# One-hot routing table: eight tokens per operation, gates in two parts, two single-pass products per token

## The reference

```
expert = take_along_axis(i_top[0] * 128 + i_top[1], pos)      # 128 experts per token (8 heads x 16)
gate   = softmax(best)
a = gelu(einsum('td,ted->te', x, u_tab[expert]))
y = einsum('te,ted->td', gate * a, v_tab[expert])
```

## Time and profile before

| | |
|---|---|
| time, median of 3 runs | 2986.67 us (2983.8 to 2988.45) |
| span of the profiled execution | 2986.7 us |
| PE busy | 2920.5 us, 98% |
| DVE busy | 1780.5 us, 60% |
| ACT busy | 1058.6 us, 35% |
| POOL busy | 799.1 us, 27% |
| `build_routing`, first product to last panel | about 796 to 1276 us |
| its 48 steps | about 796 to 1147 us |

### The profile page before, as it was taken

How to read it: one execution, slowest core, us unless ns; L and a number is a source line. 1 busy time by engine, 2 the same in 40 slices (tenths; PEclk the granted TensorE clock), 3 DMA queues, 4 the chain that set the end, 5 groups by cost and what they waited for, 6 DMA issues and landing times. The chain is left out here.

```text
span 2986.7 us, 40541 instructions
## 1 busy us (share of the span) xinstructions
PE 2920.5 (98%) x14404; PEld 2486.3 (83%) x14404; DVE 1780.5 (60%) x3707; ACT 1058.6 (35%) x1503; POOL 799.1 (27%) x502
## 2 busy tenths in 40 slices
PE   8998999999999999999999999999999999999998
PEld 6776878888788888899999997888877877788887
DVE  6586466677677771078888875444263665454422
ACT  4334332333344443233333334332133245333322
POOL 0231203444333334477676630000020320000000
PEclk9999999999999999999999999999999999999999
DMA  4222333444454554499999982233261100233332
GB/s 155 80 89 78 120 106 124 138 138 145 132 184 155 194 195 169 156 343 371 358 359 354 361 307 89 95 99 99 92 143 50 36 22 1 79 105 98 94 98 71
DMA packets 178107, 454.13 MB, mean 152 GB/s; under 512 B 21425, under 2 KB 75313, under 8 KB 176818
## 3 DMA queue, kind: packets, MB, share of 16 engines
q1 hardware_dynamic: 154146, 359.78, 36.3%
q0 software_dynamic: 22528, 67.19, 5.8%
q10 hardware_dynamic: 1296, 25.36, 2.1%
HBM read 387.06 MB, written 65.01 MB: 151 GB/s over the span
## 5 line engine op out<-in xcount | busy, mean ns | idle before, releaser
L58 PE MATMUL cb_y<-cb_g_hi,s_hi 128*128 128x384 f32 x1024 | 342.9, 335 | 2.2 <-DVEq L2294 2.2
L60 PE MATMUL cb_y<-cb_g_hi,s_lo 128*128 128x384 f32 x1024 | 342.7, 335 | 0.0
L59 PE MATMUL cb_y<-cb_g_lo,s_hi 128*128 128x384 f32 x1024 | 342.6, 335 | 0.0
L588 POOL TENSOR_TENSOR s_lo<-ex_raw,s_hi 128x1024 fp32r<-128x1024 f32 x96 | 242.3, 2526 | 345.4 <-ACT s_hi L574 345.4
L58 PE MATMUL bs_ps<-x_hi,s_hi 128*128 128x512 f32 x576 | 229.0, 398 | 2.7 <-PEq L44 2.7
L60 PE MATMUL bs_ps<-x_hi,s_lo 128*128 128x512 f32 x576 | 224.5, 390 | 0.0
L59 PE MATMUL bs_ps<-x_lo,s_hi 128*128 128x512 f32 x576 | 224.3, 389 | 0.0
L2353 POOL DMA_INDIRECT cb_rows<-in_peer_v,ex_chosen x128 | 188.8, 1475 | 68.8 <-issue 37.0
L58 PEld LDWEIGHTS cb_y<-cb_g_hi,s_hi 128*128 128x128 f32 x1024 | 192.8, 188 | 2.6 <-DVEq L2294 2.6
L59 PEld LDWEIGHTS cb_y<-cb_g_lo,s_hi 128*128 128x128 f32 x1024 | 192.8, 188 | 0.0
L60 PEld LDWEIGHTS cb_y<-cb_g_hi,s_lo 128*128 128x128 f32 x1024 | 192.7, 188 | 0.0
(11 more groups left out here) (575 smaller groups left out, 7042.8 us busy)
## 6 DMA issues: line engine op xcount, KB each, us to landing
ex_raw<-in_peer_u SPq DMA_DIRECT2D x96, 512.0 KB, 3.6
ex_raw<-in_peer_v SPq DMA_DIRECT2D x96, 512.0 KB
ffn_raw<-in_gu SPq DMA_DIRECT2D x86, 512.0 KB, 3.5
hidden<-up_out SPq DMA_DIRECT2D x128, 256.0 KB, 2.1
routing<-br_out ACTq DMA_DIRECT2D x8, 3072.0 KB, 9.2
cb_route<-routing SPq DMA_DIRECT2D x32, 768.0 KB
cb_unit<-hidden SPq DMA_DIRECT2D x128, 192.0 KB
ffn_raw<-in_down SPq DMA_DIRECT2D x44, 512.0 KB, 3.5
```

Source lines behind the costliest of these rows:

```text
L58: pe.matmul(out, w_high, x_high, start=first, stop=False, skip_group_check=skip)
L59: pe.matmul(out, w_high, x_low, start=False, stop=False, skip_group_check=skip)
L60: return pe.matmul(out, w_low, x_high, start=False, stop=last, skip_group_check=skip)
L588: eng.tensor_tensor(self.lo[:, s, :], self.raw[s], self.hi[:, s, :].bitcast(F32), ALU.subtract).then_inc(self.split, 1)
```

## The change

DVE no longer makes a one-hot per token. One operation of 8 x 128 = 1024 elements compares `iota`, repeated for the tokens, with the columns of the eight tokens, repeated for the keys, and a second does so for the rows, now without the gate. The gate is cut once for all tokens in a high part (`gate_high`, written by ACT as float32r at the start of the stage) and the rest, which DVE leaves in `packed`. `slot` takes both. Two more operations multiply the column one-hots by the high gates into `col_high` and by the low gates, in place, into `col_low`. All three one-hot tiles are float32r. PE makes two matmuls per token, row_hot by col_high and row_hot by col_low, summed in the same bank. New semaphores order the DVE operations (`gates`, `columns`, `rows`). The buffers of `Ahead` of which only the first is used before `combine_experts` are cut up; the others are allocated in that stage (`rest`).

```
-        slot = c.sb("br_slot", [P, 2, 3, B])
-        row_hot = c.sb("br_row", [P, 2, B, N_KEYS])
-        col_hot = c.sb("br_col", [P, 2, B, N_KEYS])
+        slot = c.sb("br_slot", [P, 2, 4, B])
+        row_hot = c.sb("br_row", [P, 2, B, N_KEYS], F32R)
+        col_high = c.sb("br_col_hi", [P, 2, B, N_KEYS], F32R)
+        col_low = c.sb("br_col_lo", [P, 2, B, N_KEYS], F32R)
+        gate_high = c.sb("br_gate_hi", [P, SEQ], F32R)
...
-                dve.sem_inc(S["picked"], 2)
+                dve.sem_inc(S["picked"], 4)
                 dve.sem_inc(S["hots"], 2)
+                dve.wait_ge(S["gates"], 1)
+                dve.tensor_tensor(packed[:, 2, :], packed[:, 2, :], gate_high[:].bitcast(F32), ALU.subtract
+                                  ).then_inc(S["gates"], 1)
+                dve.wait_ge(S["gates"], 2)
+                keys = iota[:].unsqueeze(1).broadcast_to([P, B, N_KEYS])
...
+                    def of_slot(x):
+                        return slot[:, k, x, :].unsqueeze(2).broadcast_to([P, B, N_KEYS])
                     dve.wait_ge(S["hots"], n + 1)
-                    dve.tensor_copy(slot[:, k], packed[:, :, at]).then_inc(S["picked"], 1)
-                    dve.wait_ge(S["picked"], n + 1 + 2)
+                    dve.tensor_copy(slot[:, k, 0:3], packed[:, :, at]).then_inc(S["picked"], 1)
+                    dve.tensor_copy(slot[:, k, 3], gate_high[:, at].bitcast(F32)).then_inc(S["picked"], 1)
+                    dve.wait_ge(S["picked"], n * 2 + 2 + 4)
                     dve.wait_ge(S["product"], n + 1)
-                    for b in range(B):
-                        dve.tensor_scalar(row_hot[:, k, b, :], iota[:], slot[:, k, 0, b:b + 1],
-                                          slot[:, k, 2, b:b + 1], ALU.is_equal, ALU.mult)
-                        last = dve.tensor_scalar(col_hot[:, k, b, :], iota[:], slot[:, k, 1, b:b + 1], None,
-                                                 ALU.is_equal)
-                    last.then_inc(S["hots"], 1)
+                    dve.tensor_tensor(col_low[:, k], keys, of_slot(1), ALU.is_equal).then_inc(S["columns"], 1)
+                    dve.tensor_tensor(row_hot[:, k], keys, of_slot(0), ALU.is_equal).then_inc(S["rows"], 1)
+                    dve.wait_ge(S["columns"], n * 2 + 1)
+                    dve.tensor_tensor(col_high[:, k], col_low[:, k].bitcast(F32), of_slot(3), ALU.mult
+                                      ).then_inc(S["columns"], 1)
+                    dve.wait_ge(S["columns"], n * 2 + 2)
+                    dve.wait_ge(S["rows"], n + 1)
+                    dve.tensor_tensor(col_low[:, k], col_low[:, k].bitcast(F32), of_slot(2), ALU.mult
+                                      ).then_inc(S["hots"], 1)
...
-                        last = pe.matmul(banks[2 * k + b // 4][:, b % 4, :], row_hot[:, k, b, :],
-                                         col_hot[:, k, b, :], start=True, stop=True)
+                        bank = banks[2 * k + b // 4][:, b % 4, :]
+                        pe.matmul(bank, row_hot[:, k, b, :], col_high[:, k, b, :], start=True, stop=False)
+                        last = pe.matmul(bank, row_hot[:, k, b, :], col_low[:, k, b, :], start=False, stop=True)
...
             @block.scalar
             def _(act):
+                act.copy(gate_high[:], packed[:, 2, :]).then_inc(S["gates"], 1)
...
-        self.route = c.sb("cb_route", [P, 2, DENSE // TOKENS, RING * TOKENS])
+        self.route = [c.sb("cb_route0", [P, DENSE // TOKENS, RING * TOKENS])]
...
+    def rest(self, c):
+        self.route += [c.sb("cb_route1", [P, DENSE // TOKENS, RING * TOKENS])]
+        self.prod += [c.sb("cb_prod1", [P, DENSE])]
+        self.g_hi += [c.sb(f"cb_g_hi{j}", [P, DENSE], F32R) for j in range(1, RING)]
+        self.g_lo += [c.sb(f"cb_g_lo{j}", [P, DENSE], F32R) for j in range(1, RING)]
```

More of the change, by code:

```diff
@@ L2077, in build_routing @@
         stream.take_banks(c, "bs")
-        S = {x: c.sem(f"br_{x}") for x in ("picked", "hots", "product", "taken", "stored0", "stored1")}
+        S = {x: c.sem(f"br_{x}") for x in ("gates", "picked", "rows", "columns", "hots", "product", "taken", "stored0", "stored1")}
         stored = [S["stored0"], S["stored1"]]
@@ L2183, in __init__ @@
         self.r_landed = [c.sem(f"cb_r_landed{s}") for s in range(2)]
-        self.prod = c.sb("cb_prod", [P, 2, DENSE])
-        self.g_hi = c.sb("cb_g_hi", [P, RING, DENSE], F32R)
-        self.g_lo = c.sb("cb_g_lo", [P, RING, DENSE], F32R)
+        self.prod = [c.sb("cb_prod0", [P, DENSE])]
+        self.g_hi = [c.sb("cb_g_hi0", [P, DENSE], F32R)]
+        self.g_lo = [c.sb("cb_g_lo0", [P, DENSE], F32R)]
         self.b0_high, self.b0_split, self.prod0_done, self.hid0_high, self.hid0_split = firsts = [
@@ L2195, in scalar @@
         act.wait_ge(self.prod0_done, 1)
-        act.copy(self.g_hi[:, 0, :], self.prod[:, 0, :]).then_inc(self.hid0_high, 1)
+        act.copy(self.g_hi[0][:], self.prod[0][:]).then_inc(self.hid0_high, 1)
     def vector(self, dve, stream):
@@ L2200, in vector @@
         dve.wait_ge(self.r_landed[0], 16)
-        dve.tensor_tensor(in_blocks(self.prod[:, 0, :]), in_blocks(self.unit[:, 0, :]),
-                          self.route[:, 0, :, :TOKENS], ALU.mult).then_inc(self.prod0_done, 1)
+        dve.tensor_tensor(in_blocks(self.prod[0][:]), in_blocks(self.unit[:, 0, :]),
+                          self.route[0][:, :, :TOKENS], ALU.mult).then_inc(self.prod0_done, 1)
         dve.wait_ge(self.b0_high, 1)
@@ L2206, in vector @@
         dve.wait_ge(self.hid0_high, 1)
-        dve.tensor_tensor(self.g_lo[:, 0, :], self.prod[:, 0, :], self.g_hi[:, 0, :].bitcast(F32), ALU.subtract
+        dve.tensor_tensor(self.g_lo[0][:], self.prod[0][:], self.g_hi[0][:].bitcast(F32), ALU.subtract
                           ).then_inc(self.hid0_split, 1)
@@ L2223, in combine_experts @@
         b_raw, b_hi, b_lo = stream.raw, stream.hi, stream.lo
+        ahead.rest(c)
         unit, route, prod, g_hi, g_lo = ahead.unit, ahead.route, ahead.prod, ahead.g_hi, ahead.g_lo
@@ L2251, in body @@
                         sp.wait_ge(prod_done, n + J)
-                        sp.dma_start(route[:, half], routing_of(routing, n, J)).then_inc(r_landed[half], 16)
+                        sp.dma_start(route[half][:], routing_of(routing, n, J)).then_inc(r_landed[half], 16)
                     sp.wait_ge(prod_done, n + 1 + J)
@@ L2275, in body @@
                     act.wait_ge(prod_done, n + 1 + 2 * J)
-                    act.copy(g_hi[:, j, :], prod[:, i % 2, :]).then_inc(hid_high, 1)
+                    act.copy(g_hi[j][:], prod[i % 2][:]).then_inc(hid_high, 1)
                 act.sem_inc(b_high, 1)
@@ L2302, in body @@
                     dve.wait_ge(hid_split, n + 1)
-                    dve.tensor_tensor(in_blocks(prod[:, i % 2, :]), in_blocks(unit[:, j, :]),
-                                      route[:, half, :, j * TOKENS:(j + 1) * TOKENS], ALU.mult
+                    dve.tensor_tensor(in_blocks(prod[i % 2][:]), in_blocks(unit[:, j, :]),
+                                      route[half][:, :, j * TOKENS:(j + 1) * TOKENS], ALU.mult
                                       ).then_inc(prod_done, 1)
@@ L2309, in body @@
                     dve.wait_ge(hid_high, n + 1)
-                    dve.tensor_tensor(g_lo[:, j, :], prod[:, i % 2, :], g_hi[:, j, :].bitcast(F32), ALU.subtract
+                    dve.tensor_tensor(g_lo[j][:], prod[i % 2][:], g_hi[j][:].bitcast(F32), ALU.subtract
                                       ).then_inc(hid_split, 1)
@@ L2391, in panel @@
                         cols = slice(f * P, (f + 1) * P)
-                        done = three_products(pe, y_ps[f][:, SPARSE:], b_hi[:, j, cols], b_lo[:, j, cols], g_hi[:, j, :],
-                                              g_lo[:, j, :], first, last, skip=True)
+                        done = three_products(pe, y_ps[f][:, SPARSE:], b_hi[:, j, cols], b_lo[:, j, cols], g_hi[j][:],
+                                              g_lo[j][:], first, last, skip=True)
                         if last:
@@ L2452, in load_ahead @@
                 sp.dma_start(ring.raw[k], down(k)).then_inc(ahead.b_landed[k], 16)
-            sp.dma_start(ahead.route[:, 0], routing_of(routing, 0, RING)).then_inc(ahead.r_landed[0], 16)
+            sp.dma_start(ahead.route[0][:], routing_of(routing, 0, RING)).then_inc(ahead.r_landed[0], 16)
             stream.wait_stored(sp, RING)
```

## The result

| | before | after |
|---|---|---|
| median of the runs, us | 2986.28 (20 runs) | 2992.62 (20 runs) |
| span of the profiled execution, us | 2986.7 | 2992.2 |

A forecast was written before the change was run, and what follows sets the result against it. The prediction took PE, busy 98% of the span, as the bound; 0 (PE) + 0 (steps) + 2.4 (start) = +2.4 us on 2986.7 gave 2989.1 us, range 2979 to 3001.

The forecast's parts named there:

- What bounds the kernel: In the 48 steps of the touched stage, PE sets the pace, at 7.26 us a step.
- PE's part: Table products in the steps: each still takes 0.107 us, paced by weight loads, so 0 us change.
- DVE's part: One-hot work per step: 4.95 us plus 2.08 from POOL, 7.03 against PE's 7.26, so 0 us cost.
- DVE's wait for PE under 12: Sign of being right: over the 48 steps DVE's wait for PE falls from 70.1 us to under 12.
- One in four one-hots at 3.3 us: Sign of being right: DVE's one-hot operations take 1.22 us, one in four about 3.3.
- The rival that DVE is the bound: DVE's step exceeds 7.26 us, at 7.35 to 7.55; 2993 to 3003 us, chance 0.20.
- The start: Stage's start: cutting the gates and POOL's interference make the first one-hots late, +2.4 us once.
- the lock: POOL's low part of a panel slows a DVE operation running beside it, by 2.08 us a step.
- The rest: Outside the steps and start: DVE's later end hidden by 134.1 us of transfer waits, moved buffers free; 0 us.
- Narrow float32r products in two passes: Table products not in a single pass or as two records, 0.21 us each; 3071 us, chance 0.07.
- The quicker load: Faster rival: table records take 0.06 to 0.08 us, gain capped by DVE; 2978 to 2986 us, chance 0.13.
- "Slower": Outcome of a measured time more than 0.2% over the kernel before, above 2992.6 us; chance 0.29.

The follow-up runs named there:

- e4: Changed kernel with the second product of each token 64 columns wide in place of 128; 2989.08 us in one run.
- e1: Changed kernel without PE's second product per token, DVE still making all four one-hot operations; 2979.13 us, ratio 0.998.
- e8: Changed kernel with one-hots, keys and both gate parts in bfloat16; 2979.02 us, ratio 0.9985.
- e10: Changed kernel with each panel's low part written by DVE between its second and third operation, not by POOL; 2992.44 us, ratio 1.0024.
- e12: Changed kernel with gates cut by DVE in the stage before and each panel's low part written by DVE behind the one-hots; 2988.61 us, ratio 1.0012.
- e9: As e8, with the token innermost in the one-hot tiles and the keys written out eight times; 3131.63 us, ratio 1.0489.
- e5: Kernel before with two more DVE operations of 1024 elements ahead of its first one-hots; 2989.78 us, ratio 1.0018.
- e6: Changed kernel with the gates cut in two by DVE at the end of the stage before; 2990.64 us, ratio 1.0023.
- e3: As e1, with POOL writing only half of each panel's low part in this stage; 2948.4 us, ratio 0.9877.
- e7: Kernel before with only its one-hots batched into three DVE operations, float32, one product per token; 2986.62 us, ratio 1.0007.
- e11: As e8, with each panel's low part written by DVE in its step and not by POOL; 2951.52 us, ratio 0.989.

## Why the prediction was right and wrong

**What bounds the kernel:** right. DVE waits for PE in 45 steps, PE for DVE once.

**PE's part, 0.107 per product and 0 in sum:** right in the mechanism. The loads set the pace (e4: same pace of a pair at half the columns in one of the two; e1: 0.105 each, but with loads and streaming left out together), and the pace depends on the type (e8: 0.056, where load and streaming weren't told apart). The size was off by 0.03 us a step, +1.1 us. It is there where POOL is silent (e10) and where PE never waited (e12), but not in e4: with 64 columns in every second product the step is 7.25 us, no longer than before. So this excess isn't the loads' alone; the narrower streaming takes it away. How isn't shown: the block is 0.034 longer than before, the panel's second matmul comes 0.024 sooner after its first, and the rest is spread over the panel in amounts under the trace's 0.01.

The Trainium skill gives some 81 ns for a pair of load and matmul of 128 columns ("TensorE: Matmul & The Clock Gate", Back-to-back issue gap). Neither type of these runs shows it: 110 ns in float32r, 56 in bfloat16, and the measurement decides.

**DVE's part, 4.95 + 2.08 = 7.03, with 0.1 to 0.2 spare:** right; 0.29 us spare in a step of 7.29, and a step of 7.06 where PE is out of the way (e1). "DVE's wait for PE under 12" came as 13.0, since PE's step is itself 0.03 longer. One in four one-hots at 3.3 us: so. The rival that DVE is the bound fell here, and was true in e1 and e8, where the gain was capped as its mechanism says.

**The start, +2.4:** the wait was right (2.70 forecast as 2.8, first product +2.34), though for another reason in the detail: the lock fell on the copy of eight elements (2.25 us from 796.39), not on a one-hot. The step that failed is to price the wait by its length alone. The clock behind it cost another 3.3 us in the profiled execution, and that is most of what the forecast lacks: with the steps' 1.1 it makes 4.4, where the median is 3.5 over the forecast. The time is still in the range because the two missing terms are small against its width, which was drawn for other rivals. That wait and clock belong together rests on e12, which took both away, and on all fourteen traces: where PE waited 1.37 to 2.71 us for its first one-hots, the clock from 800 to 812 was under 1.00 in 7 of 7; where it waited 0.89 or less with operands side by side, it was 1.00 in 6 of 6; e9 is the fourteenth. The cost doesn't follow the wait's length. Read from the first product to the 21st panel matmul behind the block, against the steady steps, it is 3.3 us in two of the seven (the changed kernel and e4) and 1.6 to 1.7 in the other five; e8 waited 2.71 us and paid 1.6. So the profile of the changed kernel may show the dearer case, and what a run pays isn't settled: the medians of e5 and e6 don't follow their profiles, within 2 to 3 us.

**The rest, 0:** right. 130.5 us from the last block on in both, and 133.4 us of DVE's wait for transfers against 134.1.

**The rivals.** Narrow float32r products in two passes: excluded by 768 records at 0.11. The quicker load: not in this type. "Slower" had 0.29, and the result is there, by 0.02% and by a mechanism that was no rival of mine.

## What to carry over

In this kernel a product with few columns costs its weight load: before its streaming is shortened, look how far apart two loads stand that follow each other, and whether a narrower type shortens those. A new wait of PE can cost more than its length (here 2.3 us of wait and 1.6 to 3.3 us for the half clock), so keep a stage's preparation away from PE's first need of it. When two engines are within 4% of each other, a gain on one shows only with the other's made together: -0.15% (within noise) and +0.24% alone, -1.1% as a pair.

## What I had not expected of the hardware

- The clock at half for 3 to 7 us behind an idle time of PE of 1.4 to 2.7 us. At the stage's border, after the same 2.72 us, it fell in some executions (e1, e3, e5, e7, e9, e11: 0.78 to 0.83 from 790 to 800) and not in the others; in e5 it cost 1.3 us, and it is a part of the runs' spread.
- POOL's lock delays small DVE instructions as much as large ones: a copy of eight elements took 2.25 us in place of 0.17.
- Operands of PE in bfloat16 at a distance of 16 bytes: 0.234 us per product instead of 0.056, and half clock behind most blocks of them, without a gap (e9).
- DVE's two-byte operations took 1.22 us in e8, where an operand is repeated in its last dimension, and 0.69, nearly twice the pace, in e9, where it is repeated in an outer one. The Trainium skill states that this pace wants a step of one in every operand ("VectorE: DVE Perf Modes", What auto-detection actually checks), and the two runs agree.
